# RMS-norm factors by two f32r products with minus ones, instead of column sums, a power and a rebuilt diagonal

## What is computed

```python
def rms_norm(x, g):
    xf = x.astype(jnp.float32)
    y = xf * lax.rsqrt(jnp.mean(xf * xf, axis=-1, keepdims=True) + EPS)
    return (y * g.astype(jnp.float32)).astype(x.dtype)
```

## Time and profile before

| | |
|---|---|
| median of 3 runs | 1120.36 us (1120.17 to 1120.57) |
| the profiled execution, its own time | 1120.9 us |
| its span | 1119.2 us |
| TensorE matmul busy | 1107.8 us, 99% |
| VectorE busy | 670.3 us, 60% |
| ScalarE busy | 495.6 us, 44% |
| GpSimd busy | 7.6 us, 1% |
| mean granted TensorE clock | 0.998 |

### The profile page before, as it was taken

The page is one execution under the profiler, slowest core; times in us unless marked ns, Lnnn a source line. Parts: engine busy times, 40 slices in busy tenths (PEclk is TensorE's granted clock), DMA queues, the critical chain, the costliest instruction groups (busy, mean ns, idle before and its releaser), DMA issues.

```text
span 1119.2 us, 15113 instructions
## 1 busy us (share of the span) xinstructions
PE 1107.8 (99%) x5430; PEld 912.9 (82%) x5430; DVE 670.3 (60%) x883; ACT 495.6 (44%) x722; POOL 7.6 (1%) x24
## 2 busy tenths in 40 slices
PE   8999999999999999999999999999999999999997
PEld 7788777788888888888888888888888888888887
DVE  6447366755777777763334557656777777763234
ACT  5557566643343444433233446644434344432231
POOL 1000000000000000000000000000000000000000
PEclk9999999999999999999999999999999999999999
DMA  5332121232332222223334221122223322233332
GB/s 196 132 114 76 57 76 57 76 100 89 99 102 99 94 94 94 84 77 102 92 103 148 75 91 58 66 85 95 94 94 99 106 94 94 77 86 96 92 101 76
DMA packets 34905, 104.58 MB, mean 93 GB/s; under 512 B 4001, under 2 KB 6194, under 8 KB 34866
## 3 DMA queue, kind: packets, MB, share of 16 engines
q1 hardware_dynamic: 34434, 103.32, 28.6%
q10 hardware_dynamic: 432, 0.73, 0.2%
HBM read 99.84 MB, written 2.10 MB: 91 GB/s over the span
## 4 chain that ended last, share of the span: by engine, by line
PE 97%; DVE 1%; DMA 1%; SPq 1%; issue 0%; ACT 0%; DVEq 0%
PE ps L1311 30%; PE ps L1312 29%; PE ps L1313 29%; PE ps L1525 1%; PE ps L1553 1%; PE ps L1650 1%; PE ps L1535 1%; PE ps L1675 1%; DMA w_raw<-w_mix 1%; PE ps L1660 1%; DVE ssq L941 1%; PE ps L1544 0%; SPq L512 0%; PE ps L1604 0%; PE ps L1613 0%
## 5 line engine op out<-in xcount | busy, mean ns | idle before, releaser
L1311 PE MATMUL ps<-h_hi,w_hi 128*128 128x512 f32 x888 | 350.2, 394 | 1.4 <-DVE h_lo L946 1.4
L1313 PE MATMUL ps<-h_hi,w_lo 128*128 128x512 f32 x888 | 345.8, 389 | 0.0
L1312 PE MATMUL ps<-h_lo,w_hi 128*128 128x512 f32 x888 | 345.8, 389 | 0.0
L650 ACT ACTIVATE w_hi<-w_raw 128x1024 fp32r<-128x1024 f32 (+2 forms) x146 | 139.0, 952 | 418.8 <-PE ps L1313 418.8
L928 DVE TENSOR_TENSOR w_lo<-w_raw,w_hi 128x1024 fp32r<-128x1024 f32 (+2 forms) x146 | 158.9, 1089 | 153.1 <-ACT w_hi L650 152.4
L1311 PEld LDWEIGHTS ps<-h_hi,w_hi 128*128 128x128 f32 x888 | 166.7, 188 | 38.2 <-issue 4.0
L1313 PEld LDWEIGHTS ps<-h_hi,w_lo 128*128 128x128 f32 x888 | 166.7, 188 | 35.1
L1312 PEld LDWEIGHTS ps<-h_lo,w_hi 128*128 128x128 f32 x888 | 166.8, 188 | 34.6 <-issue 1.2
L1311 PE MATMUL ps<-y_hi,w_hi 128*128 128x512 f32 x330 | 128.4, 389 | 0.0
L1312 PE MATMUL ps<-y_lo,w_hi 128*128 128x512 f32 x330 | 128.4, 389 | 0.0
L1313 PE MATMUL ps<-y_hi,w_lo 128*128 128x512 f32 x330 | 128.4, 389 | 0.0
(11 more groups left out here) (234 smaller groups left out, 1250.8 us busy)
## 6 DMA issues: line engine op xcount, KB each, us to landing
w_raw<-w_up SPq DMA_DIRECT2D x88, 512.0 KB, 3.2
w_raw<-w_mix SPq DMA_DIRECT2D x51, 512.0 KB, 3.3
w_raw<-w_down SPq DMA_DIRECT2D x32, 384.0 KB, 3.1
w_raw<-w_down SPq DMA_DIRECT2D x32, 320.0 KB, 2.9
x<-xT SPq DMA_DIRECT2D x8, 256.0 KB, 6.8
out<-x SPq DMA_DIRECT2D x8, 256.0 KB, 2.1
w_raw<-w_mix SPq DMA_DIRECT2D x4, 256.0 KB, 6.1
sq<-qbT SPq DMA_DIRECT2D x8, 128.0 KB, 2.3
```

The source lines that it names most:

```text
L650: s.activation(w_hi[r % SPL][:, 0:cols], w_raw[r][:, 0:cols], ACT.Copy).then_inc(w_hi_ready, 1)
L1311: mm(dst, w[0], m[0], start=first, stop=False, skip_group_check=shared)
L1312: mm(dst, w[0], m[1], start=False, stop=False, skip_group_check=shared)
L1313: return mm(dst, w[1], m[0], start=False, stop=last, skip_group_check=shared)
```

## The change

`ssq_mm`, `rms`, the power on GpSimd, `rinv_mm` and `rinv_copy` go. In their place, for each of the four norms: ScalarE rounds `ssq` to an f32r high part (`ssq_hi`), VectorE subtracts to the low part (`ssq_lo`); two f32r products with a 128 x 128 tile of minus ones give minus the sum on all partitions at once (`mean_mm`); ScalarE takes the square root with scale -1/D (`root`, function Sqrt), and VectorE the reciprocal of 128 x 512 in place (`rinv_root`). Eps comes in through the fill of `ssq`. In the mixers `rinv_col` is got by multiplying with the identity and summing (`rinv_columns`), and ScalarE waits for it right behind the root. The halves lie in blocks that are unused at the time. The warming of the Gelu table moves from ahead of the MLP's first split to behind the root. The single product stands where `rinv_mm` stood in the mixers, and where `ssq_mm` stood in the MLPs.

```diff
-            def rinv_copy(norm):
+            def ssq_hi(norm):
+
+                act.wait_ge(ssq_added, NADD * (norm + 1))
+                s.activation(ssq_parts[norm][0], ssq[:, :], ACT.Copy).then_inc(ssq_hi_ready, 1)
+
+            def root(norm):
+
                 act.wait_ge(rbc_done, norm + 1)
-                s.activation(rinv[:, :], ps[:, B_RINV, :], ACT.Copy).then_inc(rinv_ready, 1)
+                s.activation(rinv[:, :], ps[:, B_RINV, :], ACT.Sqrt, scale=-1.0 / D).then_inc(norm_root, 1)
...
+                elif name == "ssq":
+                    ssq_hi(0)
                 elif name == "rinv":
-                    rinv_copy(0)
+                    root(0)
+                    act.wait_ge(rcol_ready, 1)
...
-                act.wait_ge(warmed, layer)
-                act.wait_ge(par_loaded, 16)
-                s.activation(gelu_warm[:, :], par[:, 0:1], ACT.Gelu_apprx_tanh).then_inc(warmed, 1)
+                ssq_hi(norm)
...
                 up_hi(0, 0)
+                root(norm)
+                act.wait_ge(warmed, layer)
+                act.wait_ge(par_loaded, 16)
+                s.activation(gelu_warm[:, :], par[:, 0:1], ACT.Gelu_apprx_tanh).then_inc(warmed, 1)
                 up_hi(0, 1)
-                rinv_copy(norm)
...
-            def rms(norm):
-
-                dve.wait_ge(ssq_col, norm + 1)
-                v.tensor_scalar(var_col[:, :], ps[:, B_SSQ, 0:TT], 1.0 / D, EPS, ALU.mult, ALU.add).then_inc(var_ready, 1)
+            def ssq_lo(norm):
+
+                hi, lo = ssq_parts[norm]
+                dve.wait_ge(ssq_hi_ready, norm + 1)
+                v.tensor_tensor(lo, ssq[:, :], hi.bitcast(F32), ALU.subtract).then_inc(ssq_lo_ready, 1)
                 if 0 < norm < 2 * LAYERS:
-                    v.memset(ssq[:, :], 0.0).then_inc(ssq_added, 1)
-                dve.wait_ge(rcol_ready, norm + 1)
-                v.tensor_tensor(diag[:, :].rearrange("p (a t) -> p a t", a=TT),
-                                ident[:, :].unsqueeze(1).broadcast_to([P, TT, P]),
-                                rinv_col[:, :].unsqueeze(2).broadcast_to([P, TT, P]), ALU.mult).then_inc(diag_ready, 1)
+                    dve.wait_ge(ssq_lo_ready, norm + 1)
+                    v.memset(ssq[:, :], EPS_SHARE if norm < 2 * LAYERS - 1 else 0.0).then_inc(ssq_added, 1)
+
+            def rinv_root(norm):
+
+                dve.wait_ge(norm_root, norm + 1)
+                v.reciprocal(rinv[:, :], rinv[:, :]).then_inc(rinv_ready, 1)
+
+            def rinv_columns(n):
+
+                by_tile = diag[:, :].rearrange("p (a t) -> p a t", a=TT)
+                v.tensor_tensor(by_tile, rinv[:, :].rearrange("p (a t) -> p a t", a=TT),
+                                ident[:, :].unsqueeze(1).broadcast_to([P, TT, P]), ALU.mult).then_inc(masked, 1)
+                dve.wait_ge(masked, n + 1)
+                v.tensor_reduce(rinv_col[:, :], by_tile, AX.X, ALU.add).then_inc(rcol_ready, 1)
...
-                    rms(0)
+                    ssq_lo(0)
                 elif name == "rinv":
+                    rinv_root(0)
                     dve.wait_ge(rinv_ready, 1)
+                    rinv_columns(0)
                     a_evac0(0)
                     a_evac0(1)
...
-            def ssq_mm(norm):
+            def mean_mm(norm):
 
                 if norm == 0:
-                    pe.wait_ge(consts, N_CONSTS)
-                pe.wait_ge(ssq_added, NADD * (norm + 1))
-                for tt in range(TT):
-                    ins = mm(ps[:, B_SSQ, tt:tt + 1], ssq[:, tt * P:(tt + 1) * P], ones[:, 0:1],
-                             start=True, stop=True)
-                ins.then_inc(ssq_col, 1)
-
-            def rinv_mm(norm):
-
-                pe.wait_ge(diag_ready, norm + 1)
-                mm(ps[:, B_RINV, :], ones[:, :], diag[:, :], start=True, stop=True).then_inc(rbc_done, 1)
+                    pe.wait_ge(consts_dve, 3)
+                pe.wait_ge(ssq_lo_ready, norm + 1)
+                hi, lo = ssq_parts[norm]
+                mm(ps[:, B_RINV, :], negones[:, :], hi, start=True, stop=False)
+                mm(ps[:, B_RINV, :], negones[:, :], lo, start=False, stop=True).then_inc(rbc_done, 1)
...
                 a_unit(u_up, slot(u_up), 0, norm * KC)
-                ssq_mm(norm)
+                mean_mm(norm)
                 a_unit(u_up + 1, slot(u_up + 1), 1)
-                rinv_mm(norm)
...
-                elif name == "ssq":
-                    ssq_mm(0)
                 elif name == "rinv":
-                    rinv_mm(0)
+                    mean_mm(0)
```

More of the change, by code:

```diff
@@ L237, in trunk @@
         ones = sb("ones", [P, P])
+        negones = sb("negones", [P, P], F32R)
         diag = sq
@@ L250, in trunk @@
         negtri = s0("negtri", [P, P], F32R)
-        negones = s0("negones", [P, P], F32R)
         tri_f = s0("tri_f", [P, P])
@@ L321, in trunk @@
         y_lo = sb("y_lo", [P, FC, T], F32R)
+        ssq_parts = [tuple(t[:, n, :] for t in pair) for pair, n in
+                     (((oc_hi, oc_lo), 7), ((y_hi, y_lo), FC - 1), ((o1_hi, o1_lo), 7), ((y_hi, y_lo), FC - 1))]
         us = [sb(f"us{k}", [P, 2 + T]) for k in range(2)]
@@ L332, in trunk @@
         g_banks = ps[:, B_G:B_G + 2, :].rearrange("p b t -> p (b t)")
-        B_SSQ, B_RINV = 6, 7
+        B_RINV = 7
+        EPS_SHARE = EPS * D / P
         B_SC, B_T, B_PV = 2, 4, 6
@@ L356, in trunk @@
         x_updated = sem("x_updated")
-        ssq_col = sem("ssq_col")
-        var_ready = sem("var_ready")
+        ssq_hi_ready = sem("ssq_hi_ready")
+        ssq_lo_ready = sem("ssq_lo_ready")
+        norm_root = sem("norm_root")
+        masked = sem("masked")
         rcol_ready = sem("rcol_ready")
@@ L633, in _ @@
             assert n[0] == N_CONSTS
-            for norm in range(2 * LAYERS):
-                pool.wait_ge(var_ready, norm + 1)
-                g.tensor_tensor(rinv_col[:, :], var_col[:, :], mhalf[:, :], ALU.pow).then_inc(rcol_ready, 1)
         @block.scalar
@@ L891, in _ @@
                         b_evac(v1, CKV * CD, v_tile, b_order(0))
+                elif name == "ssq":
+                    ssq_hi(2)
                 elif name == "rinv":
-                    rinv_copy(2)
+                    root(2)
+                    act.wait_ge(rcol_ready, 2)
                 elif name == "s_exp":
@@ L959, in res_split @@
                 add_sq(norm, c)
-            def rms(norm):
-                dve.wait_ge(ssq_col, norm + 1)
-                v.tensor_scalar(var_col[:, :], ps[:, B_SSQ, 0:TT], 1.0 / D, EPS, ALU.mult, ALU.add).then_inc(var_ready, 1)
+            def ssq_lo(norm):
+                hi, lo = ssq_parts[norm]
+                dve.wait_ge(ssq_hi_ready, norm + 1)
+                v.tensor_tensor(lo, ssq[:, :], hi.bitcast(F32), ALU.subtract).then_inc(ssq_lo_ready, 1)
                 if 0 < norm < 2 * LAYERS:
-                    v.memset(ssq[:, :], 0.0).then_inc(ssq_added, 1)
-                dve.wait_ge(rcol_ready, norm + 1)
-                v.tensor_tensor(diag[:, :].rearrange("p (a t) -> p a t", a=TT),
-                                ident[:, :].unsqueeze(1).broadcast_to([P, TT, P]),
-                                rinv_col[:, :].unsqueeze(2).broadcast_to([P, TT, P]), ALU.mult).then_inc(diag_ready, 1)
-            v.memset(ssq[:, :], 0.0).then_inc(ssq_added, 1)
+                    dve.wait_ge(ssq_lo_ready, norm + 1)
[9 more added lines that the diff above has]
+                v.tensor_reduce(rinv_col[:, :], by_tile, AX.X, ALU.add).then_inc(rcol_ready, 1)
+            v.memset(ssq[:, :], EPS_SHARE).then_inc(ssq_added, 1)
             def half_lo(u, half):
@@ L1145, in later_stages @@
                         y_lo_part(i, k - 4)
+                ssq_lo(norm)
                 up_lo(0, 0)
@@ L1149, in ffn @@
                     v.memset(us[k][:, 0:2], 0.0).then_inc(halo, 1)
-                rms(norm)
+                rinv_root(norm)
                 up_lo(0, 1)
@@ L1230, in _ @@
                 elif name == "ssq":
-                    rms(2)
+                    ssq_lo(2)
                     v.memset(k1[:, :, 0:CHUNK], 0.0).then_inc(c_pad, 1)
@@ L1236, in _ @@
                 elif name == "rinv":
+                    rinv_root(2)
                     dve.wait_ge(rinv_ready, 3)
+                    rinv_columns(1)
                     a_evac1(0)
@@ L1476, in last_rbc @@
             def last_rbc(half):
-                pe.wait_ge(diag_ready, 2 * LAYERS + half + 1)
+                pe.wait_ge(diag_ready, half + 1)
                 mm(ps[:, B_RBC[half], 0:TH], ones[:, :], diag[:, tok_half(half)],
@@ L1636, in _ @@
                         a_unit(U_MIX1 + i, slot(U_MIX1 + i), a_bank1(a), 2 * KC if i == 0 else None, span)
-                elif name == "ssq":
-                    ssq_mm(2)
                 elif name == "rinv":
-                    rinv_mm(2)
+                    mean_mm(2)
                 elif name == "s":
```

## The result

| | before | after |
|---|---|---|
| median of 10 runs each | 1120.17 us (1119.57 to 1120.81) | 1123.64 us (1120.83 to 1125.79) |
| ratio, 95% interval | | 1.0029 (1.0021 to 1.0036) |
| the profiled execution | 1120.9 us | 1125.79 us |
| its span | 1119.2 us | 1124.0 us |
| mean granted clock | 0.998 | 0.992 |

The kernel is 3.5 us slower, a little over the 0.2% that can be told. The number is in the range given (1118.2 to 1124.4), but it is not where the forecast stood (1121.1, no change): it is near the price of rival 2 (1124.1). It is also above 1122.6, the line that the prediction drew for "slower by over 0.2%", a case to which it gave 0.27. The spread is new too: 5 us where the kernel before has 1.2. The profiled execution is the slowest of the ten; the ten granted clocks lie between 0.992 and 0.996, in step with the times (0.992 for the three of 1125.2 and more, 0.996 for 1120.83).

The account below looks back on a forecast made before the run. TensorE's products were taken to bound the kernel, with 97% of the chain. Mixer 0 +2.97, mixer 1 +0.54 and the MLPs -2.82 gave +0.7 us on 1120.36: 1121.1 us, no change that can be told, range 1118.2 to 1124.4.

Parts of the forecast that it names:

- rival 2: TensorE's gaps in the mixers lower the granted clock, slowing products behind them: 3 us more, 1124.1 us; chance 0.13.
- TensorE's saving, 1.41 us a norm: Each norm drops column sums (0.95 us) and broadcast product (0.91) for a 0.45 us pair, where no wait comes in.
- MLPs hidden: In both MLPs the halves are ready 0.1 us ahead and the root and reciprocal chain is hidden: -2.82 us together.
- Reciprocal 3.3 us by a slope from two rows: VectorE's 512-column reciprocal, carried on from rows of 2 and 8 columns at 6.2 ns a column: 3.3 us.
- The upper end of 4.4 us: Upper bound for VectorE's 512-column reciprocal, by a slope a third steeper, 8.3 ns a column.
- rival 1: The reciprocal takes 4.4 us and both mixers hang on it: 2 x 1.1 us more, 1123.3 us; chance 0.13.
- rival 4: The reciprocal is as cheap as a plain operation: sum -3.9 us, 1116.5 us; chance 0.05.
- Mixer 1, +0.54: Window scores in mixer 1 start at 629.1 instead of 628.57, behind the longer chain and take-outs: +0.54 us.
- Mixer 0, first score product +1.0: In mixer 0 the first score product starts at 34.05 instead of 33.01, behind later take-outs: +1.0 us.
- Mixer 0, +2.97 at the running sums, by SP's queue: Swap DMAs wait for a take-out and delay unit 6's load; the second low half's product starts at 52.35, not 49.37.
- rival 3: The chain through unit 6's load doesn't decide; mixer 0 costs only +1.0: -1.2 us, 1119.2 us; chance 0.11.
- Rival 5: Each ScalarE table switch costs 2.66 us, 1.38 more than the row: +3.8 us in all, 1124.9 us; chance 0.02.

Follow-up runs that it names:

- fillers: Changed kernel plus products with unread results in TensorE's two gaps, 11 in mixer 0 and 8 in mixer 1: 1121.16 us, ratio 1.0007 to the kernel before.
- fillers in mixer 0 alone: Changed kernel plus 11 products with unread results in mixer 0's gap, none in mixer 1: 1121.47 us, ratio 1.0012 to the kernel before.
- Ln and Exp: Changed kernel with columns behind the take-outs and ScalarE's Ln, Exp replacing root and reciprocal in all four norms: 1115.05 us, ratio 0.9956 to the kernel before.

## Why the prediction was right or wrong

- **TensorE's saving, 1.41 us a norm**: right. -1.41 and -1.40 us between marks, the pair 0.45 to 0.46, and -2.5 us in the run with the MLPs alone, where two norms should give -2.8.
- **MLPs hidden**: right, the halves were in time by 0.2 us (0.1 forecast).
- **Reciprocal 3.3 us by a slope from two rows**: right, 3.352 us, or (3352 - 203) / 504 = 6.25 ns a column. The upper end of 4.4 us and rival 1 with it are out, and so is rival 4. The Trainium skill (VectorE: DVE Perf Modes, "First, the fixed hardware budget") gives the divide a repeat count of 8; that this means 8 full cycles a column, as the upper end had it, is out by the same number. The Trainium skill (Trainium Kernel Development and Optimization, "NeuronCore Architecture") gives VectorE 0.96 GHz; by that the 6.25 ns are an estimated 6 cycles.
- **Mixer 1, +0.54**: right for the wait (+0.53, gap 1.86 us).
- **Mixer 0, first score product +1.0**: +0.78 in the profile. It came less late because the chain started 0.3 us earlier: the additions of squares ended at 23.74, not at 24.03, and TensorE's wait ahead of unit 3 was 0.37 us, where some 0.7 were expected.
- **Mixer 0, +2.97 at the running sums, by SP's queue**: the mechanism is right and its size too, but only where the clock holds (+2.98 with fillers), and rival 3 is out there. That the sum agrees to 0.01 us is partly luck: the first score product came 0.18 us earlier than forecast (33.87, not 34.05), and the way from it to the second mark was as much longer. In the profiled run of the changed kernel this chain did not decide, since the products ahead of it were slow enough to cover it.
- **The step that failed** is the weighing of rival 2. I set it at 0.13 because "before that gap TensorE had been only partly busy, which in mixer 0 it is not". Dense products ahead of the gap did not protect the clock: all ten runs of the changed kernel have a mean of 0.992 to 0.996, where all but 4 of 47 runs of the kernel before in the experiments' rounds have 0.997 or 0.998, and the fillers give it back. The price of 3 us was near the measured 3.5 - 0.7 = 2.8 over the forecast, but it is 6.7 us of lost product time in the slowest run. Net it is less. Against the run with fillers the second mark of the running sums is 54.91 - 52.35 = 2.6 us later, since the low clock took the place of the two waits, and mixer 1 adds 1.6. The rival's price was the forecast plus 3, with the waits and the slow products side by side, so that it came close to the median is partly luck. With that rival the likeliest case, the forecast would have been slower, near 1124. The measured time is inside my range only because I stretched the range to that rival's price; the forecast's own range ended at 1122.2.
- **Rival 5**, 1.38 us more for each table load: out. The Trainium skill (ScalarE: Activation LUTs, "What ACT_TABLE_LOAD costs") adds a drain of that length to each switch. The traces do not agree: a load follows its predecessor and is followed by its successor within 0.02 us where nothing else is waited for (41.20 to 42.50 in mixer 0, 26.73 to 28.02 with Ln and Exp).

## What to carry to other kernels

A wait on TensorE is priced by its length only as long as the clock stays up; a new gap of 1.3 to 2.6 us, as here, can double the time of the products behind it, in some runs of a program and not in others. Where such a gap can't be closed, products into an unused bank are a cheap way to find out what it costs, and to avoid it. And a chain that is twice as long on an engine with time to spare costs only where somebody waits for its end: the same change gains in the MLPs and loses in the mixers.

## What the runs showed of the hardware

- The granted clock went from 2.4 to 1.2 GHz behind gaps of TensorE of 2.63, 1.86 and 1.31 us that followed dense products. It fell at the end of the gap of 2.63 us, and about a microsecond behind the end of the other two, when TensorE was busy again. Behind the gap of 2.63 us in the profiled run it stayed there for some 10 us of unbroken products, behind that of 1.86 us for 3.4 us; in the profiled run with fillers in mixer 0 alone the same gap of 1.86 us left it at full.
- A mean clock of 0.995 or 0.996 also turned up in 4 of 47 runs of the kernel before, which has none of these three gaps, and in one of ten with the MLPs alone. No trace shows why.
- A reciprocal on VectorE of 128 x 512 in f32 takes 3.352 us, 6.25 ns a column, and a plain operation of that size 0.69 us.
- Ln, a table load and Exp of 128 x 512 on ScalarE are together 2.54 us, and so shorter than Sqrt on ScalarE and that reciprocal (3.98 us).
